# Second feed-forward of a hybrid encoder: block sums in PSUM, weight sums shared by GpSimd and VectorE, operand splits spaced by two products

## The reference, cut to what matters

```python
def swiglu(h, w1, w3, w2):
    return (jax.nn.silu(h @ w1) * (h @ w3)) @ w2
...
    h = h + swiglu(rmsnorm(h, norm_ffn[i]), ffn_w1[i], ffn_w3[i], ffn_w2[i])
```

## Time and profile before

| | before |
|---|---|
| median of 3 runs | 2732.88 us (2732.68 to 2734.39) |
| the profiled execution: its own time, its span | 2730.89 us, 2729.1 us |
| TensorE busy in the span | 97% |
| rounds 1 to 10 of the second feed-forward | 2056 to 2480 us of the span |
| plain units, 20 down units | 2480 to 2505 us, 2505 to 2702 us |

### The profile page before, as it was taken

One profiled execution on the slowest core, in us unless ns is written; L12 is line 12 of the kernel. 1 busy time (PEld: TensorE's weight loads), 2 busy tenths in 40 slices (PEclk: granted clock), 3 DMA queues, 4 the chain that ended last, 5 costly groups with the idle time before them and its releaser, 6 DMA issues.

```text
span 2729.1 us, 39028 instructions
## 1 busy us (share of the span) xinstructions
PE 2655.9 (97%) x14503; PEld 2181.2 (80%) x14503; DVE 1641.6 (60%) x2133; ACT 972.3 (36%) x1680; POOL 1673.5 (61%) x1371
## 2 busy tenths in 40 slices
PE   8999999999999999999999999999999999999997
PEld 7888888799999999999877545554777777777886
DVE  4544444447444444445877876676467888776555
ACT  4333433424222222223331556655233333332114
POOL 5655655546555555557344667665458888787664
PEclk9999999999999999999999999999999999999999
DMA  8212222512111111111333000001213433336562
GB/s 227 65 58 61 61 63 63 201 47 63 50 49 46 46 46 46 47 52 52 110 82 61 17 1 16 16 1 62 98 47 106 145 135 135 140 131 253 225 270 77
DMA packets 215615, 236.82 MB, mean 87 GB/s; under 512 B 21496, under 2 KB 183712, under 8 KB 210992
## 3 DMA queue, kind: packets, MB, share of 16 engines
q1 hardware_dynamic: 198768, 176.53, 21.0%
q10 hardware_dynamic: 16704, 58.39, 5.3%
HBM read 168.40 MB, written 61.21 MB: 84 GB/s over the span
## 4 chain that ended last, share of the span: by engine, by line
PE 73%; DVE 8%; POOL 7%; DMA 7%; issue 3%; SPq 1%; ACT 1%; ACTq 0%; POOLq 0%; DVEq 0%
PE PS L1212 20%; PE PS L1141 12%; PE PS L1465 9%; PE PS L1269 9%; PE PS L1743 6%; PE PS L1757 5%; DMA down_raw<-in_ffn_w 3%; DMA g_operands<-gls 3%; PE PS L1517 2%; PE PS L1553 2%; PE PS L1683 2%; PE PS L1493 2%; POOL wl L863 2%; POOL down_lo L931 2%; PE PS L1346 1%
## 5 line engine op out<-in xcount | busy, mean ns | idle before, releaser
L837 POOL TENSOR_TENSOR wh<-wraw,ones 128x512 fp32r<-128x512 f32 x120 | 143.6, 1197 | 369.1 <-PE PS L1141 187.3
L2396 ACT ACTIVATE pf<-PS 128x512 f32<-128x512 f32 (+1 forms) x288 | 169.9, 594 | 161.8 <-PE PS L1743 160.5
L3093 DVE TENSOR_REDUCE nmx<-PS 128x1 fp32r<-128x1044 f32 x128 | 156.8, 1228 | 102.0 <-PE PS L1683 102.0
L840 POOL TENSOR_TENSOR wl<-wraw,wh 128x512 fp32r<-128x512 f32 x120 | 189.9, 1582 | 9.4
L2530 DVE TENSOR_TENSOR h<-PS,h 128x1044 f32<-128x1044 f32 (+1 forms) x96 | 119.3, 1242 | 110.7 <-PE PS L1269 110.7
L1212 PE MATMUL PS<-uh,wh 128*128 128x512 f32 (+1 forms) x400 | 156.8, 392 | 27.0 <-POOL wl L863 26.8
L863 POOL TENSOR_TENSOR wl<-upraw,wh 128x512 fp32r<-128x512 f32 x81 | 106.4, 1313 | 122.0 <-ACT wh L1879 122.0
L1082 POOL TENSOR_TENSOR accp<-accp,pf 128x1024 f32<-128x1024 f32 x64 | 152.7, 2386 | 18.0 <-ACT pf L2396 17.0
L2259 ACT ACTIVATE pt<-PS 128x512 f32<-128x512 f32 x128 | 75.8, 592 | 233.5 <-PE PS L1517 226.9
L2530 DVE TENSOR_TENSOR h<-h,PS 128x512 f32<-128x512 f32 x160 | 108.0, 686 | 81.4 <-PE PS L1346 79.5
L1757 PE MATMUL PS<-pf,vg 128*64 128x512 f32 x576 | 155.2, 618 | 0.0
(11 more groups left out here) (387 smaller groups left out, 7875.2 us busy)
## 6 DMA issues: line engine op xcount, KB each, us to landing
g_operands<-gls ACTq DMA_DIRECT2D x63, 512.0 KB, 2.6
wraw<-in_ffn_w SPq DMA_DIRECT2D x91, 256.0 KB, 2.9
even_group<-g_operands SPq DMA_DIRECT2D x21, 1024.0 KB, 12.2
upraw<-in_ffn_w SPq DMA_DIRECT2D x83, 256.0 KB, 3.0
odd_group<-g_operands SPq DMA_DIRECT2D x14, 1024.0 KB, 13.3
wraw<-in_a_w_qkv SPq DMA_DIRECT2D x48, 256.0 KB, 2.9
down_raw<-in_ffn_w SPq DMA_DIRECT2D x40, 256.0 KB, 6.8
biasb<-bias_shifts SPq DMA_DIRECT2D x128, 72.0 KB, 2.6
```

The source lines that it names most:

```text
L840: nc.gpsimd.tensor_tensor(wl[:, slot, 0:w], wraw[:, slot, 0:w], wh[:, slot, 0:w].bitcast(F32), ALU.subtract).then_inc(s_wrd, 1)
L2396: nc.scalar.activation(pf[q, s % PB, e, :], PS[q, 6 + e, :], ACT.Exp).then_inc(s_gex, 1)
L3093: nc.vector.tensor_reduce(nmx[:, i:i + 1], PS[:, set_:set_ + 3, 0:CW], AX.XY, ALU.max, negate=True).then_inc(s_mr, 1)
```

## The change

It does five things, all in the second feed-forward.

1. VectorE writes the joined blocks back to PSUM: c + u3 into bank b, u3 - d into bank d, c + u2 into bank c. The multiplications by rstd and into the gated rows then read one input from PSUM. The 128x1024 multiplication of row 1 becomes two of 128x512.
2. S3 and S4 move from GpSimd to VectorE (`weight_sums`). S4 is written over S2, no longer over A12.
3. The order on VectorE and ScalarE is written anew. On ScalarE a `split_hi` and the `spill` of the same piece are apart by more products, and splits do not stand ahead of the hi parts that they stood ahead of before.
4. At the end, the additions of the first two plain results move ahead of an operand sum and a split. TensorE's wait for the second bank set of the plain units is for the row that reads it (`s_gm`).
5. SyncE issues, for down groups 1 to 4, three operands, the weights of the group's first unit, and then the other four operands.

```diff
@@ SyncE, fetch_phased
-                        for j in range(GOPS):
+                        for j in (B11, T1, T4):
                             operand(q, j)
                         for e in range(4 * q, 4 * q + 4):
                             sp.wait_ge(s_wrd, U_DOWN + 2 * (e - 1))
                             weights(e)
+                            if e == 4 * q:
+                                for j in (T2, B21, B22, T3):
+                                    operand(q, j)
@@ GpSimd, phased
                         lo(o + 3, 0, r[A22])
-                        po.wait_ge(s_wrd, n + 2)
-                        sum_of(r[A11], r[A11], r[A21], ALU.subtract, s + 3)
                         lo(o + 4, 0, r[A11])
                         lo(o + 5, 0, r[A12])
-                        po.wait_ge(s_wrd, n + 6)
-                        sum_of(r[A12], r[A12], r[S3], ALU.subtract, s + 4)
-                        lo(o + 6, 0, r[A12])
+                        lo(o + 6, 0, r[S3])
@@ ScalarE, phased
                         up(k, 3)
+                        if r > 1:
+                            split_hi(p - 1, 6)
+                        up(k, 4)
                         if r == 1:
                             act.wait_ge(s_tl, 8)
-                        else:
-                            split_hi(p - 1, 6)
-                        up(k, 4)
...
                         else:
-                            split_hi(p, 1)
                             spill(p, 0)
                             up(k, 6)
+                            split_hi(p, 1)
+                            up(k, 7)
                             spill(p, 1)
+                            up(k + 1, 1)
                             split_hi(p, 2)
-                            up(k, 7)
...
@@ VectorE, phased
+                    def weight_sums(k):
+                        r, n = QROLES[k % 5], us + 7 * k
+                        a11, a21, a12, s2 = (rb[1][r[i]] for i in (A11, A21, A12, S3))
+                        dve.wait_ge(s_wrd, n + 2)
+                        tt(a11, a11, a21, ALU.subtract, s_wsum)
+                        dve.wait_ge(s_wrd, n + 3)
+                        dve.wait_ge(s_xr[r[A12]], 16 * (LOADS[r[A12]] + loads_of(r[A12], k)))
+                        tt(s2, a12, s2, ALU.subtract, s_wsum)
...
+                    def row1_sums(k):
+                        a, b, c, d = QBANK[1][k % 2]
+                        dve.wait_ge(s_un, us + 7 * k + 5)
+                        tt(u3_, ps(b), s1_, ALU.add, s_u3)
+                        dve.wait_ge(s_u3, tb + k + 1)
+                        tt(ps(b), ps(c), u3_, ALU.add, s_c22)
+                        tt(ps(d), u3_, ps(d), ALU.subtract, s_c21)
...
                     split_lo(last, 0)
+                    plain_add(0)
                     operand_sum(last, 0)
                     split_lo(last, 1)
-                    plain_add(0)
+                    plain_add(1)
                     operand_sum(last, 1)
-                    plain_add(1)
@@ TensorE, plain_sets
                     elif m == 1:
-                        pe.wait_ge(s_c21, tb + QUADS)
+                        pe.wait_ge(s_gm, mb + ROWS_MADE - 1)
```

More of the change, by code:

```diff
@@ L1940, in up @@
                             summed(sums + 4 * k + 4)
[L1941 removed]
+                        hi(us, o, r[(A22, A11, S3, A22, A11, A12, S3)[j - 1]])
                     def plain(d):
@@ L2552, in g_lo, with sums @@
                     tt(g2l[l][g][:, b, tok], a_[:, b, tok], g2h[l][g][:, b, tok].bitcast(F32), ALU.subtract, s_gr)
-                def nothing():
-                    return None
-                def sums(n, o3, o5, t, q, between=nothing):
+                def sums(n, o3, o5, t, q):
                     a, b, c, d = QBANK[l][q]
@@ L2561, in sums @@
                     tt(u2_, ps(b), s1_, ALU.add, s_u2)
-                    between()
                     dve.wait_ge(s_un, n + o5)
@@ L2565, in sums, with gate_quad @@
                     dve.wait_ge(s_u3, t)
-                def gate_quad(n, last, t, a_=at[l], between=nothing):
+                def gate_quad(n, last, t):
                     a, b, c, d = QBANK[l][0]
@@ L2572, in gate_quad @@
                         tt(a_[:, 1, third], ps(EBANK[0][1]), rstd[:, third], ALU.mult, s_e1)
-                    sums(n, op(l, last, 3), op(l, last, 5), t, 0, between)
+                    sums(n, op(l, last, 3), op(l, last, 5), t, 0)
                     tt(a_[:, 1, right], ps(c), u3_, ALU.add, s_c22)
@@ L2587, in gate_quad, with gated_quad @@
                     tt(a_[:, 0, right], a_[:, 0, right], rstd[:, right], ALU.mult, s_ar)
-                def gated_quad(n, o, last, t, a_=at[l], between=nothing, behind=nothing):
+                def gated_quad(n, o, last, t):
                     a, b, c, d = QBANK[l][1]
@@ L2594, in gated_quad @@
                         tt(a_[:, 1, third], a_[:, 1, third], ps(EBANK[1][1]), ALU.mult, s_e1)
-                    sums(n, o3, o5, t, 1, between)
+                    sums(n, o3, o5, t, 1)
                     tt(c22s[l], ps(c), u3_, ALU.add, s_c22)
@@ L2601, in gated_quad @@
                     tt(a_[:, 1, left], a_[:, 1, left], u3_, ALU.mult, s_gm)
-                    behind()
                     dve.wait_ge(s_un, n + o6)
@@ L2650, in phased @@
                         plain_round = r == FIT - 1
[L2652 to L2670 removed]
+                        a, b, c, d = QBANK[1][0]
                         if not plain_round:
@@ L2673, in phased @@
                             operand_sum(p, 0)
-                        gate_quad(us + 7 * k, 0, tb + k + 1, t, between_gate)
+                        weight_sums(k)
+                        two_products(k)
                         if not plain_round:
-                            split_lo(p, 2)
-                        gate_row(1, 2 * r + 1, t)
-                        gate_row(0, 2 * r + 2, t)
+                            split_lo(p, 1)
+                            operand_sum(p, 1)
+                        row1_sums(k)
+                        dve.wait_ge(s_c22, tb + k + 1)
+                        tt(t[:, 1, right], ps(b), rstd[:, right], ALU.mult, s_ar)
+                        dve.wait_ge(s_c21, tb + k + 1)
+                        tt(t[:, 1, left], ps(d), rstd[:, left], ALU.mult, s_ar)
                         if plain_round:
@@ L2681, in phased @@
                         else:
-                            split_lo(p, 3)
-                        dve.wait_ge(s_sr, k0 + 2 * r + 2)
-                        gated_quad(us + 7 * (k + 1), 1, 0, tb + k + 2, t, between_gated, behind_row)
+                            split_lo(p, 2)
+                        dve.wait_ge(s_un, us + 7 * k + 6)
+                        tt(t[:, 0, left], ps(a), rstd[:, left], ALU.mult, s_c11)
+                        row0_sum(k)
+                        tt(t[:, 0, right], ps(c), rstd[:, right], ALU.mult, s_ar)
+                        if plain_round:
+                            g_lo(0, gs_before(last) - ROWS_MADE, 0, ats[PLAIN_AT % 2])
+                        else:
+                            split_lo(p, 3)
+                        gate_row(1, 2 * r + 1, t)
+                        if not plain_round:
+                            operand_sum(p, 2)
+                        gate_row(0, 2 * r + 2, t)
+                        k += 1
+                        a, b, c, d = QBANK[1][1]
+                        weight_sums(k)
+                        two_products(k)
+                        if not plain_round:
+                            split_lo(p, 4)
+                            split_lo(p, 5)
+                        row1_sums(k)
+                        dve.wait_ge(s_sr, k0 + 2 * r + 2)
+                        dve.wait_ge(s_c22, tb + k + 1)
+                        tt(t[:, 1, right], t[:, 1, right], ps(b), ALU.mult, s_b22)
+                        dve.wait_ge(s_c21, tb + k + 1)
+                        tt(t[:, 1, left], t[:, 1, left], ps(d), ALU.mult, s_gm)
+                        dve.wait_ge(s_un, us + 7 * k + 6)
+                        tt(t[:, 0, left], t[:, 0, left], ps(a), ALU.mult, s_c11)
+                        if not plain_round:
+                            operand_sum(p, 3)
+                        row0_sum(k)
+                        tt(t[:, 0, right], t[:, 0, right], ps(c), ALU.mult, s_gm)
+                        if not plain_round:
+                            split_lo(p, 6)
                     def plain_add(m):
```

57 lines of the change are left out of this document (25 added, 32 removed).

## The result

| | before | after |
|---|---|---|
| median | 2733.52 us (2732.68 to 2734.39, 4 runs) | 2694.04 us (2691.33 to 2696.15, 4 runs) |
| ratio | 1 | 0.9855, 95% interval 0.9838 to 0.9872 |
| profiled execution | 2730.89 us | 2694.75 us, span 2692.4 us |

The change makes the kernel 1.45% faster. Put on the median that the prediction started from, that is 0.9855 x 2732.88 = 2693.3 us. The forecast was 2700 with 2694 as the low end: the direction came true, and the likeliest case in kind, but the gain was forecast too small. The changed kernel was measured again beside the experiments, with 2698.02 us (2695.48 to 2699.01, 4 runs) against 2733.07, a ratio of 0.9873 (0.9857 to 0.989), which is 2698.2 us on the same median. So the forecast size lies inside the interval of the second measurement and not of the first, and both say more than 32 us.

The account below looks back on a forecast made before the run. TensorE's waits, mostly for GpSimd's lo parts, were taken as the bound. Rounds 30.8, plain units 2.7 and reloads 2.3 make 35.8; less 3, 2730.89 - 32.8 = 2698.1, plus 2.0 for the median: 2700 us, range 2694 to 2720.

Parts of the forecast that it names:

- the likeliest case: Whole kernel: all steady waits of TensorE in the rounds go; 2700 us, own range 2694 to 2707, chance 0.60.
- (a): Rounds: the port shared by VectorE and GpSimd, not the order, sets the round; no change, 2728 us; chance 0.05.
- (b): Rounds: one wait of about 1 us a round stays, at product 5 or 2; 13 us back, 2713; chance 0.23.
- (c): Value quads: S3 made at 11.9 us, 3.0 over its 8.9 deadline; 2733, or 2750 if TensorE's clock falls; chance 0.12.
- The rule that the prediction set against itself: VectorE and GpSimd share an SBUF read port, so moving the weight sums between them would give nothing.
- slacks of 1.3 and 1.5 us: Rounds: time to spare for S3 in the value quad (1.3) and for the chain to product 2 (1.5).
- the reserve: 3 us set against the gain for single waits where slow instructions of 1.1 us each exceed the slacks.
- Rounds: Rounds 1 to 10: steady waits, the time beside them and 1.7 us of low clock go, 30.8 us in sum.
- The waits (22.3): Rounds: all 25 steady waits of TensorE for lo parts go, 25.9 - 3.6 = 22.3 us; the first wait stays.
- what lies beside them (6.8): Rounds: each wait costs 0.27 us beside its own length, 25 x 0.27 = 6.8 us.
- Plain units: Plain units: the 1.8 us wait for the first addition and most of 1.7 us low clock go; 2.7 of 3.5 kept.
- Reloads: Down units: waits at two group starts go with interleaved loads, 1.8 + 2 x 0.27 = 2.3 us.

Follow-up runs that it names:

- sums_in_sbuf: Changed kernel with only the block sums of row 1 and row 0 written to SBUF again: 2698.15 us, ratio 0.9877.
- psum_only: Kernel before with only the block sums in PSUM; weight sums, split order, plain units and reloads as before: 2707.85 us, ratio 0.9897.
- old_order_both: Kernel before with weight sums on VectorE and block sums in PSUM; split order, plain units and reloads as before: 2696.19 us, ratio 0.987.
- P alone: The same run as psum_only, block sums in PSUM as the only edit to the kernel before: 2707.85 us, ratio 0.9897.
- plain_order: Changed kernel with the third and fourth additions of the plain units each one place earlier: 2694.89 us, ratio 0.9854.

## Where the prediction was right, and the step that failed

**Bound and direction.** TensorE's waits were what could be given back, and they were. Rounds of 38.58 us were forecast as 38.6 to 39, 3.6 us of waits for lo parts as under 8, 0.68 us for a write to PSUM (measured 0.70), and the third weight sum at 7.0 and 7.6 us of the gate and the value quad (6.7, and 7.6 with 7.9 in the last quad). GpSimd's sums for unit 8 start 63.9 us behind the first down unit instead of 71.7. The rivals (a) and (b) are not seen; (c) would need the sum 1.3 us later, as the runs with idle additions show. The rule that the prediction set against itself, that sums moved between GpSimd and VectorE give nothing, is half true here: alone they took 18.5 us off the rounds, beside the other two edits 0.1 us.

**The size.** By the profiled executions: forecast 32.8, found 36.1 us. The mechanism was right and the size was off. The step that failed is the last one, "Against this I set 3 us for single waits where slacks of 1.3 and 1.5 us are less than what two or three slow instructions take": none of the waits came back. The slack was not eaten, because the queues repeat themselves: the sum is made at 7.60 to 7.63 us in nine value quads and at 7.90 in the last. Even in sums_in_sbuf, where that slack is gone, 1.7 us came back and not 3. Without the reserve the sum was 35.8. The terms:

- *Rounds*, 30.8 without the reserve, measured 33.9. The waits (22.3) and what lies beside them (6.8) are right. Of the missing 3 us, 1.1 are low clock behind the start wait, of which the changed kernel's profile happens to have less (the first quad takes 24.63 us, before 25.70; in the second profile of the changed kernel it takes 25.78): that is luck. The others are delays under 0.3 us each, which no row lists as a wait and which I had not summed. All 3 us are less than the 4.1 by which two executions of the old rounds differ.
- *Plain units*, 2.7 forecast, 0.7 measured, and in the second profile a loss of 0.9. The wait did not go; it grew from 1.81 to 2.75 us, and the 0.7 are low clock that happened to stay away in the first profile. psum_only and old_order_both, with the old place of the additions, have waits of 1.8 and 0.6 us and the same 24.8 us. The text asked what is late next, but for TensorE at the second addition and at down unit 1. The third addition, behind four VectorE instructions, was not looked at. It is the one term that was wrong in kind. Moving it up moved the wait on once more.
- *Reloads*, 2.3 forecast, 2.36 in the run that has them alone. Beside faster rounds they are worth more: with old reloads the stretch up to the end of TensorE's last wait is 202.45 us (old_order_both) to 203.77 (psum_only) against 198.59, which is 3.9 to 5.2 us. Why is not shown.
- *The two ends* that no edit touches brought +1.9 and about -1.8 us and cancel.
- *The median* was set 2.0 us above the profiled execution. In the first measurement it came out 0.7 below it, in the second 0.3 above. So 2693.3 lies just outside the range of 2694 to 2720 and 2698.2 inside it: which side of 2694 it fell is chance, the needless reserve is not. Of the 6.6 us between the forecast gain of 32.9 and the 39.5 of the first medians, 3.3 are in the profiled executions and the rest is how these lie to the medians. The range's low end allowed for all of the 37 us and about 2 more (2732.88 - 37 = 2695.9), and had no room for a spread of medians beside that.

**The reading of the causes.** This was less right than the number. The prediction gave the steady waits to the weight sums on GpSimd and the long ones to the spills, and to the block sums only 6.6 us of VectorE's time. By the eight combinations, the largest single cause was the block sums (28.3 of 34 us), any two edits are enough, and the sum on GpSimd or the order of the splits can each be left as they were at a cost of 0.1 us or less. The spills need not be moved either: P alone ended ScalarE's waits for them. Why VectorE's speed reaches that far is read from the rows, as is the loop; that any two edits are enough is measured. The timeline of GpSimd ahead of a wait was read rightly, but it shows one stretch of a loop. That all parts were late there did not tell which part, shortened, would let go.

## What to carry to other kernels

When several queues feed each other in a loop, an edit has no price of its own: here three edits worth 28, 18 and 11 us alone give 34 together, and taking out any one costs 0 to 1.7. Test such a change by leaving each part out and by making each alone; the first view by itself would have called every edit nearly worthless, the second would have promised 58 us. And where a wait is taken away, lay out the next four or five instructions of the queue, not the next one. And compare the length of a loop's turns, not only the waits that are listed: 0.15 us lost ten times was in no row of waits.

## What the runs showed of the hardware

The price of a VectorE instruction with two SBUF inputs depends on where it falls in a GpSimd instruction, and the other way round. In the changed kernel, GpSimd's timeline, then VectorE's:

```profile
2201.79 1.66 POOL L866 TENSOR_TENSOR wl<-upraw_b,wh 128x512 fp32r<-128x512 f32 x1 [1.18 <-ACT wh L1878]
...
2201.09 1.21 DVE L2530 TENSOR_TENSOR at<-at,rstd 128x1024 f32<-128x1024 f32 x1
2202.22 1.78 DVE L2530 TENSOR_TENSOR at_odd<-at_odd 128x512 f32<-128x512 f32 x1
```

VectorE's first ends at 2202.30; GpSimd's lo part, issued at 2201.79, ends at 2203.45, some 1.2 us after that, which is nearly its own 1.29. VectorE's next ends at 2204.00, 0.55 after GpSimd's, where it takes 0.68 alone. They take turns, to within 0.14 us each. So in the plain units of plain_order a 512-wide sum took 2.88 us, beside a GpSimd lo part of 1024 columns:

```profile
2459.25 4.84 POOL L930 TENSOR_TENSOR down_lo<-down_raw,down_hi 128x1024 fp32r<-128x1024 f32 x2 [0.19 <-ACT down_hi L1979]
```

(two of 2.42 us; the first ends at 2461.67, VectorE's sum at 2462.40). The Trainium skill, "SBUF — State Buffer", section "SBUF: two separate sides", has the rule: whichever of the two starts first gets the shared pair of ports for the whole instruction, and the other fully blocks. The traces agree to the 0.14 us above. What it means for a mean price is that 1.78 us is not the price of such an instruction but 0.68 and the rest of whatever GpSimd has begun. A 512-wide instruction with an input from PSUM is outside of this (0.68 to 0.70 in the groups above), so the block sums in PSUM shortened six VectorE instructions a round and, by the same reading, stopped them from holding up GpSimd too. That would explain why this edit alone was worth the most; it is argued from the rows, no run separates the two effects.
